# More of the modulation on TensorE between the turned tokens, fewer chunks on GpSimd, and the sinks as one more key

## What is computed

```
c_act = jax.nn.silu(c)
ada = c_act @ w_ada[layer] + b_ada[layer]
shift1, scale1, gate1, shift2, scale2, gate2 = jnp.split(ada, 6, axis=-1)

h = modulate(rms_norm(x, norm1_g[layer]), shift1, scale1)
proj = h @ w_in[layer]
...
sink_col = jnp.broadcast_to(sink_f[None, :, None, None], (B, N_HEADS_A, WIN_BLOCK, 1))
p = jax.nn.softmax(jnp.concatenate([s, sink_col], axis=-1), axis=-1)[..., :span]
...
x = x + gate1[:, None, :] * (mixed @ w_out[layer])

h2 = modulate(rms_norm(x, norm2_g[layer]), shift2, scale2)
x = x + gate2[:, None, :] * peer(h2, w_query[layer], sub_keys[layer],
                                  u_experts[layer], v_experts[layer])
```

## Time and profile before

| | us |
|---|---|
| median of 3 runs | 2360.06 |
| lowest and highest run | 2357.99, 2364.99 |
| time of the profiled execution | 2354.66 |
| its span in the trace | 2352.7 |
| PE busy in the span | 2092.2 (89%) |
| POOL busy | 984.7 (42%) |
| first gather issued by POOL | 369.74 |

### The profile page before, as it was taken

The page is one execution under the profiler, slowest core; times in us unless marked ns, Lnnn a source line. Parts: engine busy times, 40 slices in busy tenths (PEclk is TensorE's granted clock), DMA queues, the critical chain, the costliest instruction groups (busy, mean ns, idle before and its releaser), DMA issues. The chain is left out here.

```text
span 2352.7 us, 21614 instructions
## 1 busy us (share of the span) xinstructions
PE 2092.2 (89%) x6760; PEld 1147.8 (49%) x6760; DVE 1315.9 (56%) x2973; ACT 925.5 (39%) x2366; POOL 984.7 (42%) x609
## 2 busy tenths in 40 slices
PE   5979898888898998887799989999878998999999
PEld 4767543333333333333233333333335554888887
DVE  5144346777777777785644454444466553432432
ACT  3444433444445444443333343333334443321321
POOL 0797003656654565653567765667510000000000
PEclk8999799999999999999999999999987998999999
DMA  6543526999999999999999999999921002233231
GB/s 271 199 149 108 176 110 244 420 421 416 410 414 375 421 421 416 410 415 395 421 420 419 421 421 402 416 421 421 381 84 48 1 1 72 90 97 100 90 108 54
DMA packets 118019, 651.65 MB, mean 277 GB/s; under 512 B 10872, under 2 KB 29200, under 8 KB 46096
## 3 DMA queue, kind: packets, MB, share of 16 engines
q0 software_dynamic: 73728, 536.90, 55.4%
q1 hardware_dynamic: 41232, 108.04, 13.0%
q10 hardware_dynamic: 2944, 5.33, 0.6%
HBM read 648.13 MB, written 2.10 MB: 276 GB/s over the span
## 5 line engine op out<-in xcount | busy, mean ns | idle before, releaser
L834 PE MATMUL bank<-ring,diag 128*128 128x512 f32 x2048 | 995.0, 612 | 149.9 <-ACT diag L1324 147.9
L529 POOL DMA_INDIRECT ring<-in_uv,idx x512 | 812.8, 1587 | 655.3 <-PE bank L834 238.8
L1874 DVE CUSTOM_DVE_ANT_0 zjunk<-ring,h 128x1024 bf16<-128x1024 f32 x512 | 627.3, 1225 | 455.2 <-DMA ring<-in_uv,idx 454.9
L834 PEld LDWEIGHTS bank<-ring,diag 128*128 128x128 f32 x2048 | 368.9, 191 | 712.3 <-ACT diag L1324 426.6
L1318 ACT ACTIVATE zg<-z 128x1 f32<-128x1 f32 x512 | 103.4, 202 | 695.1 <-DVE z L1874 694.7
L1324 ACT ACTIVATE diag<-ident,weight 128x128 f32<-128x128 f32 x512 | 205.5, 401 | 16.8
L800 PE MATMUL bank<-w_inb,hTb 128*128 128x512 f32 (+1 forms) x320 | 145.5, 557 | 0.7 <-ACT hTb L1312 0.7
L2088 DVE TENSOR_TENSOR ml_lo<-mlp_raw,ml_hi 128x2048 fp32r<-128x2048 f32 x32 | 73.4, 2293 | 114.4 <-ACT ml_hi L1466 114.4
L767 PE MATMUL bank<-w_q,h2T 128*128 128x512 f32 x256 | 131.6, 605 | 3.6 <-ACT h2T L1238 3.6
L1466 ACT ACTIVATE ml_hi<-mlp_raw 128x2048 fp32r<-128x2048 f32 x32 | 61.1, 1908 | 121.8 <-PE bank L561 107.6
L559 PE MATMUL bank<-hTm_hi,ml_hi 128*128 128x512 f32 x256 | 100.9, 394 | 1.6 <-DVE hTm_lo L2083 1.6
(11 more groups left out here) (249 smaller groups left out, 2637.3 us busy)
## 6 DMA issues: line engine op xcount, KB each, us to landing
ada_w<-in_w_ada SPq DMA_DIRECT2D x24, 1024.0 KB
mlp_raw<-in_w_up SPq DMA_DIRECT2D x16, 1024.0 KB, 5.4
mlp_raw<-in_w_down SPq DMA_DIRECT2D x16, 1024.0 KB, 5.1
win_raw<-in_w_in SPq DMA_DIRECT2D x9, 1024.0 KB, 9.2
w_inb<-in_w_in SPq DMA_DIRECT2D x8, 1152.0 KB
w_q<-in_w_query SPq DMA_DIRECT2D x8, 1024.0 KB, 9.5
ring<-in_uv,idx POOLq DMA_INDIRECT x512
x<-in_x SPq DMA_DIRECT2D x8, 512.0 KB, 7.6
```

The lines of the kernel that those rows point to most:

```text
L529: e.indirect_dma_start(ring[n % RING], None, a["uv"], bass.IndirectOffsetOnAxis(ap=idx[i][:, j:j + 1], axis=0)).then_inc(s[f"d_ring{n % RI ...
L834: t = e.matmul(bank[2 * (i % 2) + half], diag[n % 4], ring[n % RING][:, 1024 + 512 * half:1536 + 512 * half], start=(j == 0), stop=(j == 127))
L1874: e.tensor_tensor_reduce(out=zjunk, in0=ring[n % RING][:, 0:1024], in1=h2[:, i, :], scale=1.0, scalar=0.0, op0=ALU.mult, op1=ALU.add, accu ...
```

## The change

Chunks 8 to 11 are made by PE alone, one before each tile of tokens is turned, so POOL and ACT have twelve chunks, 12 to 23, and ACT multiplies for six of them where it did for eight. Their loads move forward in SP's queue, between the first loads of `w_in`. The totals of the other chunks stand at other steps; that of chunk 12 stands ahead of step 0's pieces. The copies of totals by ACT and DVE come two steps after the total's step. The sink is copied by DVE into one more column of the scores before each of the 32 units with a sink, and ACT's exponential takes it along; the three operations of each tile's end are gone. `prob` grows from 384 to 400 words.

```
-ADA_PE = (1, 3, 5, 7)
-ADA_ACT = (8, 9, 10, 12, 14, 16, 18, 20)
-ADA_STEP = dict(zip(range(8, 24), (0, 1, 2, 4, 5, 8, 9, 12, 14, 17, 18, 22, 23, 27, 29, 33)))
-MULTIPLY_AT = {u + half: (n, half) for n, u in ((12, 2), (14, 5), (16, 10), (18, 15), (20, 19)) for half in (0, 1)}
+ADA_PE = (1, 3, 5, 7, 8, 9, 10, 11)
+ADA_ACT = (12, 13, 14, 16, 19, 22)
+ADA_STEP = {12: 0, 13: 2, 14: 4, 15: 6, 16: 8, 17: 10, 18: 13, 19: 15, 20: 18, 21: 22, 22: 24, 23: 28}
+MULTIPLY_AT = {u + half: (n, half) for n, u in ((16, 2), (19, 11), (22, 19)) for half in (0, 1)}
...
@@ SP: loads
-            for c in range(3):
-                load_win(c)
-            q.wait_ge(s["v_hn"], 8)
-            q.wait_ge(s["a_ss1"], 4)
+            load_win(0)
             load_ada(8)
             load_ada(9)
-            e.dma_start(slot[0], a["norm2_g"].partition_broadcast(128)).then_inc(s["d_g2"], 16)
+            load_win(1)
+            load_ada(10)
+            load_ada(11)
+            load_win(2)
...
@@ POOL: ada_columns, and its order
-                q.wait_ge(s["p_ada"], max(n - 1, 8))
+                q.wait_ge(s["p_ada"], max(n - 1, 12))
...
             win_low(0)
             win_low(1)
-            ada_columns(8)
+            ada_columns(12)
+            ada_columns(13)
             win_low(2)
-            ada_columns(9)
+            ada_columns(14)
             win_low(3)
-            for n in (10, 11, 12):
-                ada_columns(n)
+            ada_columns(15)
+            ada_columns(16)
             win_low(4)
...
@@ PE
             for i in range(NT):
+                ada_total(i + 8)
                 for g in (0, 1):
...
+                if u == 0:
+                    ada_total(ADA_AT[u])
                 for _ in range(PIECES[u] if u < len(PIECES) else 0):
                     next(pieces)
-                if u in ADA_AT:
+                if u > 0 and u in ADA_AT:
                     ada_total(ADA_AT[u])
...
@@ ACT
-                P = prob[u % 4][:, 0:hi - lo]
+                P = prob[u % 4][:, 0:hi - lo + 1 - g]
                 q.wait_ge(s["v_s"], 2 * u + 2)
+                if g == 0:
+                    q.wait_ge(s["v_sink"], u + 1)
...
             for i in range(NT):
+                shift_chunk(8 + i)
                 for g in (0, 1):
...
-                if u >= 3 and UNITS[u - 3][1] == 0 and UNITS[u - 3][2] == 7:
-                    i = UNITS[u - 3][0]
-                    q.wait_ge(s["v_o"], 4 * i + 1)
-                    e.activation(nm[:, i, 0:8], nm[:, i, 0:8], ACT.Exp).then_inc(s["a_sink"], 1)
...
@@ DVE
+                    e.tensor_copy(prob[u % 4][:, hi - lo:hi - lo + 1], sink[:, h:h + 1]).then_inc(s["v_sink"], 1)
...
-                if g == 0:
-                    e.tensor_tensor(nm[:, i, cs], sink, nm[:, i, cs], ALU.add).then_inc(s["v_o"], 1)
-                    q.wait_ge(s["a_sink"], i + 1)
-                    e.tensor_tensor(rs[:, i, cs], rs[:, i, cs], nm[:, i, cs], ALU.add).then_inc(s["v_o"], 1)
-                    q.wait_ge(s["v_o"], n)
```

More of the change, by code:

```diff
@@ L68, in ada_place, with ada_bank @@
 def ada_place(n):
-    return n if n < 8 else 8 + n % 2
+    return n % 8 if n < 12 else 8 + n % 2
+def ada_bank(n):
+    return n % 2 if n < 12 else 7
 def ada_use(n):
-    return 1 if n < 8 else (n - 8) // 2 + 2
+    return n // 8 + 1 if n < 12 else (n - 12) // 2 + 3
 def ada_summed(n):
-    return 9 * (n // 2 + 1) if n < 8 else sum(4 if m in ADA_ACT else 5 for m in range(8, n + 1))
+    return 9 * (n // 2 + 1) if n < 8 else sum(4 if m in ADA_ACT else 5 for m in range(12, n + 1))
 def item_chunk(n):
@@ L170, in out_done @@
 def out_done(t):
-    return 4 * t + 4 if t < 4 else 16 + 2 * (t - 4) + 2
+    return 2 * t + 2
 def mix_bank(i):
@@ L409, in load_query @@
                 e.dma_start(w_q[n][half], a["w_query"][n][:, 2048 * half:2048 * half + 2048].rearrange("p (k n) -> p k n", k=4)).then_inc(s[f"d_wq{n}"], 16)
-            for n in range(4):
+            for n in range(3):
                 load_bias(n)
@@ L415, in _ @@
                 load_x(i)
+            for n in (3, 4, 5):
+                load_bias(n)
             q.wait_ge(s["p_item"], 22)
@@ L418, in _ @@
                 e.dma_start(keysT[n], a["keysT"][:, 1024 * n:1024 * n + 1024]).then_inc(s["d_keys"], 16)
-            for n in range(4, 8):
+            for n in (6, 7):
                 load_bias(n)
@@ L569, in ada_total @@
             def ada_total(n):
-                b, p = bank[n % 2 if n < 8 else 7], ada_place(n)
-                before = n - 2 if n < 8 else n - 1
-                if n == 8:
+                p, total = ada_place(n), bank[ada_bank(n)][:, 0:256]
+                before = n - 2 if n < 12 else n - 1
+                if n == 12:
                     name, value = copied(5)
@@ L582, in ada_total @@
                     for k in range(8):
-                        e.matmul(b[:, 0:256], cb[:, k, :], ada_w[p][:, k, :], start=(k == 0), stop=False)
+                        e.matmul(total, cb[:, k, :], ada_w[p][:, k, :], start=(k == 0), stop=False)
                     r = ADA_ROW[p]
-                    e.matmul(b[:, 0:256], one[r:r + 1, :], brow[p], start=False, stop=True).then_inc(s["p_ada"], 1)
+                    e.matmul(total, one[r:r + 1, :], brow[p], start=False, stop=True).then_inc(s["p_ada"], 1)
                 else:
                     q.wait_ge(s["v_ada" if n < 8 else "g_ada"], ada_summed(n))
-                    e.matmul(b[:, 0:256], one, ada_sum[n // 2 % 2 if n < 8 else 2 + n % 2], start=True, stop=True).then_inc(s["p_ada"], 1)
+                    e.matmul(total, one, ada_sum[n // 2 % 2 if n < 8 else 2 + n % 2], start=True, stop=True).then_inc(s["p_ada"], 1)
             q.wait_ge(s["v_const"], 2)
@@ L1075, in shift_chunk @@
                     q.wait_ge(s["v_ada"], ada_summed(6))
-                e.activation(dst[:, Q[n % 4]], bank[n % 2 if n < 8 else 7][:, 0:256], ACT.Copy).then_inc(s["a_shift"], 1)
+                e.activation(dst[:, Q[n % 4]], bank[ada_bank(n)][:, 0:256], ACT.Copy).then_inc(s["a_shift"], 1)
             def split_win(c):
@@ L1124, in _ @@
             split_win(1)
-            ada_products(8, range(8))
+            ada_products(12, range(8))
             def copy_item(n):
@@ L1552, in scale_chunk @@
                 q.wait_ge(s["p_ada"], n + 1)
-                e.scalar_tensor_tensor(g, bank[n % 2 if n < 8 else 7][:, 0:256], 1.0, g, ALU.add, ALU.mult).then_inc(s["v_scale"], 1)
+                e.scalar_tensor_tensor(g, bank[ada_bank(n)][:, 0:256], 1.0, g, ALU.add, ALU.mult).then_inc(s["v_scale"], 1)
             def turned(h, i, g):
```

61 lines of the change are left out of this document (34 added, 27 removed).

## The result

The changed kernel takes 2336.61 us, median of 4 runs (2332.91 to 2340.85); beside it the kernel before took 2360.67 (4 runs, 2357.99 to 2364.99). The ratio is 0.9897 with a 95% interval of 0.9874 to 0.992: 24 us faster, between 19 and 30. The forecast was 2349, 11 us faster, within a range of 2336 to 2362. So the sign came out as forecast, and the gain is twice the forecast one.

The account below looks back on a forecast made before the run. PE was taken to wait on POOL's pace and POOL's hold on DVE. PE's running lag (time after less before) went +5.2, +3.0, +12.0, +4.9, +0.5, -9.9, -11.3; from the median 2360.06 that gave 2349 us, range 2336 to 2362.

Parts of the forecast that it names:

- steps 1 and 2: Front and first items: chunk matmuls at full clock, lag +5.2; warm start gives back 2.2 us, lag +3.0.
- step 3: Kernel step 0: PE waits 6.2 us for POOL before item 6, then 1.5 us of slow clock; lag +12.0.
- steps 4 and 5: Kernel steps 1 to 14: shorter ACT waits, 1.8 us wait for POOL before item 10; lag +4.9, then +0.5.
- step 6: Kernel steps 15 to 21: 7.67 us sink wait, 2.3 of slow clock and one total go, -10.4; lag -9.9.
- step 7: Kernel steps 22 to 36: 1.47 us wait and two totals go, +1 for POOL's total in step 28; lag -11.3.
- step 8: 32 one-column sink copies on DVE at 0.15 us, 4.8 us in sum; 0 taken on PE, at most 4.8.
- what is won or lost up to there is taken to shift the rest as it is: From the first gather, at 369.74 us before, onward: the lag carries over unchanged; nothing booked behind step 36.
- the wait in step 0 isn't there: Rival: front and step 0 cost at most 6 us together and PE stays warm; 2341 us, chance 0.12.

Follow-up runs that it names:

- e7: Changed kernel with win_low(3) ahead of chunk 14, chunk 12's total behind step 0's pieces, bias loads 8 and 9 ahead of the query weights; 2329.89 us, ratio 0.9886.
- e9: Changed kernel with win_low(3) ahead of chunk 14 and also win_low(4) ahead of chunk 16 on POOL; 2326.79 us, ratio 0.987.
- e3: Changed kernel with win_low(3) ahead of chunk 14 in POOL's queue; 2327.32 us, ratio 0.987.
- e8: The kernel before, unchanged, profiled a second time; 2354.7 us (one run).
- e2: Chunk part alone: the changed kernel with the sinks as before, bias load order still changed; 2345.09 us, ratio 0.9943.
- e4: Changed kernel with the sink copy written as a maximum of the column with itself, so two SBUF inputs; 2359.64 us, ratio 1.0.
- e6: Kernel before with bias loads 8 and 9 issued ahead of the first query weights; 2356.22 us (one run).
- e1: Sink part alone: the kernel before with the sink as one more key and nothing else; 2352.7 us, ratio 0.9964.
- e5: Kernel before with only SP's bias loads 3 to 5 issued ahead of the keys; 2358.35 us (one run).
- e10: Changed kernel with SP's bias loads back in the old order; 2333.63 us (one run).

## Why the prediction was right in sign and half in size

- **Front (steps 1 and 2).** Right. At the full clock, as taken; 4.2 us of chunk records and 1.1 of transposes for each tile, as worked out. The first item came 1.4 us earlier than forecast. Of the 2.2 us that a warm start should give back, 0.8 came in this execution, with a mean granted clock of 0.94 from 61 to 88 us; in e7 and e9, where it is 1.00, all 2.2 came. e3 has the same program as e7 and e9 up to there and 0.94 as well, so this is of the execution.
- **Step 0 (step 3).** Right, to 0.5 us: 6.17 where 6.2 was forecast, released by POOL's low part. e3 shows that this wait, and no other, stood there: without it PE is 7.9 to 9.2 us further by step 14.
- **Steps 1 to 14 (steps 4 and 5).** Right: +4.5 for +4.9 and +0.1 for +0.5, with the waits of 1.49 and 0.91 us. In the single steps it was less exact: step 3 kept 0.87 and not 1.1, and step 12 kept 0.91 where nothing was left in the ledger.
- **The sinks (step 6).** The wait is gone, as forecast, but the term was undersized: -10.4 forecast, -12.8 measured by step 24. It left out a wait of 0.96 us for ACT at 162.5 us, which e8 also has and the changed kernel hasn't, and took too little slow clock. e2 adds that the booking to the sinks was too narrow: the new queue of POOL alone takes the same wait down to 1.51 us.
- **Step 28 (step 7).** Right: +1 forecast, 1.07 measured.
- **The sink copies (step 8).** Right: 146 ns and no wait, near the 153 to 155 of the row they were taken from. The rule that the prediction named from the Trainium skill, page SBUF — State Buffer, section "SBUF: two separate sides", is borne out here by e4 for its case of two SBUF inputs (8.10 us). For its other case, a 2-port mode, nothing is settled: the fp32 copy of one column from SBUF to SBUF waits in none of 32 places, 26 of them beside a running POOL instruction, but no trace shows which mode it ran in.
- **The failed step** is the sentence "what is won or lost up to there is taken to shift the rest as it is". Steps 37 to 58 did not shift as they were. The kernel before has in step 48 a wait of DVE for a bias load, worth 5 us with the slow clock behind it (e6), and in the kernels with the new chunks it shrinks or goes: the stretch, put at nothing in the sum, is 4.3 us shorter from the first profile of before to that of after, and 3 us on average over all of them. The first query adds 0.3 to 1.6 us, by its clock. I had read the stretch up to 240 us row by row and not the 90 us behind it, where the row of 3.84 us on DMA stood in the same profile.
- **The rest of the gap is between executions.** By two profiles each, the change is worth 18.9 us (2354.66 and 2354.7 against 2332.91 and 2338.63); by medians 24 and 22. Both profiles of before are of its faster executions: the 38 runs of it beside the experiments go from 2353.53 to 2369.44 with a median of 2359.6, and the slower ones have the lower mean clock, 0.962 at 2353.53 and 0.955 at 2369.44. So the forecast's own way, the sum from one profile set against a median, leaves out some 4 us that the kernel before loses in its slower executions. Where, only other profiles hint. e6 has the program of before up to step 44 and loses 4.4 us more at the third sink by step 32. e1 and e5 have it from the first gather on, and behind that point they fall back by 5.9 and 6.3 us against the profile of before, 3.5 and 3.9 of them behind the last gather. Of a slower execution of the kernel before itself there is no profile.

Together, by the mean of two profiles each: 13.5 us by step 36 where 11.3 was forecast, 4.3 from there to the first gather (3.4 in steps 37 to 58, 0.9 in the first query) in place of 0, 1 behind it, and some 4 in executions that were not profiled. What stays open is why the same two loads of query weights land 1 us sooner with the new chunks: e10 excludes the order of the bias loads, and e2 shows that the chunk part does it without the sinks. The rival "the wait in step 0 isn't there" forecast a time that is nearer than the forecast's, 2341, by a cause that the trace refutes.

## What to carry to other kernels

Follow the lag past the last edited instruction, to the next place where two engines or a DMA meet: a wait there of a few us, such as the bias load of step 48, can vanish when the work ahead of it moves. Where PE feeds from GpSimd's queue, the order of that queue is worth as much as its load: one exchanged pair of entries gave 6 to 9 us, against 24 for the whole change. And a small VectorE instruction with two SBUF inputs beside a busy GpSimd is worth a rewrite as a one-input instruction, even if there are four times as many of them (32 copies for 8 additions).

## What the runs showed of the hardware that was not expected

- A VectorE instruction with two SBUF inputs didn't get in between two GpSimd instructions that follow one another without a pause: 8.10 us on one column, over a 4.53 and a 3.59 us instruction (4.53 us from 173.13, the next from 177.63). It ended with the second, behind which POOL paused for 0.08 us (181.22 to 181.30). The 8.22 us of the earlier trace rows end in the same way, at 175.51, with a multiply that ends at 175.49. So what such an instruction waited here was a whole unbroken run of GpSimd's queue, not what was left of one instruction. All fourteen of e4 that took over 0.3 us end within 0.03 us of a GpSimd instruction's end, and none ends between two that follow one another without a pause.
- The same column as a one-input copy took 142 to 156 ns in all 32 places.
- The kernel before repeats itself within 0.3 us for 370 us in two executions, but e6, the same program up to step 44, is 1.1 us off at step 0 and 5.2 by step 32. The changed kernel has two profiles 4.3 us apart at the first gather: the 16 matmuls of the first query alone took 8.57 and 9.86 us.
- Two loads of 1 MB each, issued one behind the other, took 8.5 to 8.7 us to land in four profiles and 7.4 to 7.8 in seven others, in the same place of SP's queue. Why is open.
